# First merge weights ahead of the sample state outputs, and state transfers split by branch, on SyncE's queue

## The chip, the cores and the metric

The kernel runs on one core of a Trainium2 chip. The metric is the device time of one execution in microseconds (us); the time before is the median of three runs.

## The reference

Two layers of a hybrid decoder are applied to a prompt of 512 tokens and to a sample group of 8 sequences with 4 tokens each, with the same weights. Each layer is a half-step SwiGLU FFN, a token mixer and a second half-step FFN, each with a norm before and after. What matters here is the mixer:

```python
h = rmsnorm(x); proj = h @ w_in          # three branches and the gate logits
o_gdn, s_gdn_new = gated_delta_rule(...)  # state 4 heads x 128 x 128 per sequence
o_gla, s_gla_new = gla(...)               # state 4 x 64 x 128
o_ssd, s_ssd_new = ssd(...)               # state 8 x 64 x 128
gates = sigmoid(gate_logits + b_merge)
merged = gates[0]*(o_gdn @ w_br_gdn) + gates[1]*(o_gla @ w_br_gla) + gates[2]*(o_ssd @ w_br_ssd)
x += rmsnorm(merged @ w_out)
```

The prompt starts from zero states; the sample starts from eight given states per branch. The new states of both are outputs of the kernel.

## The kernel before, in words

Prompt and sample columns lie side by side in tiles of 128 x 544 (512 + 32). Every large product is made from fp32 weights in three passes (high x high, high x low, low x high): SyncE (SP) loads a weight block into one of four `raw` slots, GpSimd (POOL) splits it into `wh` (L494) and `wl` (L496), of which there are two slots each, and TensorE (PE) multiplies (L531, L533, L535). `lo_done` counts split blocks and frees raw slots, `blk_done` counts blocks that PE has used and frees `wh` and `wl`, and `raw_full` tells POOL that a block has landed. All engines run the same sequence of blocks.

The mixer of a layer runs in this order: the input projection (80 big loads over both layers), then a recurrent stage in which no weight is split, then 48 merge blocks of 6 k-tiles, then the output projection. In the recurrent stage each engine follows an order written out by hand (`TENSOR_ORDER`, `SCALAR_ORDER`, `VECTOR_ORDER`) over four prompt chunks and then one step for the sample. The work tiles of that stage lie over the ring of weights: `ssd_places` and the norm tiles over `raw`, `gla_places` over `wh` and `wl`. So no merge weight may be loaded before this work is over. The sample's states lie in `states` (gdn) and in columns of `proj` (`gla_states`, `ssd_states`) that the prompt's last chunk has finished with.

The semaphores `g_["s"]`, `l_["s"]` and `s_["s"]` count finished steps of the three branches: at `CHUNKS + 1` the prompt's last state of this layer is final, at `STEPS + 1` the sample's are. VectorE (DVE) writes them: L2123 (gla), L1993 (gdn) for the prompt; L2166 (gla), L2275 (ssd), L2038 (gdn) for the sample. SP's queue in a layer is, in its own order: `save_conv`, `load_states` (L431 waits for all three branches, L433 issues gdn, gla, ssd; `st_in`), `save_prompt_states` (L420, `st_prompt`), `save_states` (L438 waits and L439 issues gdn, gla, ssd; `st_out`), a wait for `st_prompt` (L465), and then the merge blocks (L401), each once `lo_done` says that its raw slot is free.

On the other side, PE's sample products wait for `st_in` at L806, L1002 and L1125 (products at L811, L1006, L1128). DVE waits for `st_prompt` at L2351 ahead of the first `hl` of the merge (L2354). PE waits for the last step of all three branches (L1216) ahead of the first merge block, and then runs six units per turn, of two blocks each: the gate's columns, then a branch's. Each unit takes two pairs of PSUM banks; from the third unit on it waits for `sg_done` and `mac_done`, which start at 2. For a unit DVE scales the gate (`sg`, L2389), ScalarE (ACT) takes its sigmoid (L1702), DVE multiplies (`mac`, `mt`, L2394) and adds (L2398). `sg`, `mt` and `mac` lie over the gdn states, so both ACT (L1695) and DVE (L2377) wait for `st_out`, all three state outputs, before the first unit.

Of the kernel before, what the change touches and what calls it, by code (L numbers as in the profile page):

```python
# [13 lines left out]
KD = D_MODEL // P  # L14
# [3 lines left out]
CHUNKS = SEQ // C  # L18
STEPS = CHUNKS + 1
# [37 lines left out]
B_MERGE = B_PROJ + 4 + 40  # L57
# [3 lines left out]
RAW, SPLIT = 4, 2  # L61
# [90 lines left out]
def trunk(nc, io):  # L152
    ctx = ExitStack()
    with ctx:
# [5 lines left out]
        def sem(name):  # L160
            return ctx.enter_context(nc.semaphore(name))
# [62 lines left out]
        def work(name, k, units=1, dt=F32):  # L224
            return at(name, R + 2048 * k, [P, 512 * units], dt)


        (kn, qn, _, _, eg, dd, aa, att, al_, xx, xt, pp, rt, rr, uu, kd, gs) = (
            work(f"g{i}", i) for i in range(17))
        kqg = at("kqg", R + 2048 * 2, [P, 2, 512])  # L230
# [35 lines left out]
        ls = gla_prompt["s"]  # L266
# [9 lines left out]
        ss_ = ssd_prompt["s"]  # L276
# [50 lines left out]
        def halves(ap):  # L327
# [21 lines left out]
        g_ = {s: sem("g_" + s) for s in (  # L349
            "xx qx xtt bc d dx brb sq ss ln rs qk kk kt eg kg at atb xi kd al p pc q x "  # L350
            "tb cx sk rt rtt r up u o oc su sm s bx mp ma sa").split()}
        l_ = {s: sem("l_" + s) for s in (
            "rc z zt a g1 gk b bt qk qe dl d1 d2 ml at cp vc vtp vt kdp kt o oc su sm s mp ma sa").split()}
        s_ = {s: sem("s_" + s) for s in (
            "bc d dx sa st tr ea ce att xd xe bt y yo yc su sm s mp skc wide").split()}
        zeroed = sem("zeroed")
        st_in = [sem(f"st_in{b}") for b in range(3)]
        st_prompt, st_out = sem("st_prompt"), sem("st_out")
# [14 lines left out]
        def value(eng, v):  # L373


            if not isinstance(v, int):
                eng.compute_val(v)
                eng.wait_ge(started, 1)
            return v
# [11 lines left out]
        @block.sync  # L391
        def _(sp_):
            sp_.dma_start(cst[:], io["cst"]).then_inc(loaded, 16)
            sp_.dma_start(x[:], io["x"].rearrange("p (k t) -> p k t", k=KD)).then_inc(loaded, 16)
            sp_.dma_start(wpre[:], io["prm"].rearrange("a p n -> p a n")[:, :, F1PRE:F1PRE + KD]).then_inc(loaded, 16)

            def blocks(layer, first, i, nks, source):

                for j, nk in enumerate(nks):
                    sp_.wait_ge(lo_done, value(sp_, layer * BLOCKS + i * len(nks) + (first + j + 1)))  # L400
                    sp_.dma_start(raw[:, j % RAW, 0:nk, :], source(j)).then_inc(raw_full[j % RAW], 16)  # L401

            def tiles(name, index):
                return io[name][bass.ds(index, 1)].rearrange("a p (k m) -> p (a k) m", m=P)

            def ups(layer, which, first, i):
                blocks(layer, first, i, (KD,) * 4, lambda j: tiles("up", layer * (2 * UPS) + i * 4 + (which * UPS + j)))

            def ffn(layer, which, first):
                with sp_.Fori(1, KF // 2) as i:  # L410
                    ups(layer, which, first, i)
                k0 = np.cumsum((0,) + DOWN_K)
                with sp_.Fori(0, 2) as i:
                    blocks(layer, first + UPS, i, DOWN_K * 4,
                           lambda j: tiles("down", layer * (2 * KD) + i * 4 + (which * KD + j // 3))
                           [:, k0[j % 3]:k0[j % 3 + 1], :])

            def save_prompt_states(layer):
                for name, cols, live in (("gdn", 512, gs), ("gla", 256, ls), ("ssd", 512, ss_)):
                    sp_.dma_start(io["out_p_" + name][bass.ds(layer, 1)].rearrange("a p n -> (a p) n"), live[:, 0:cols]).then_inc(st_prompt, 16)  # L420

            def sample_states(kind, layer):

                return ((io[kind + "gdn"][bass.ds(layer, 1)].rearrange("a p b n -> (a p) b n"), states[:, :, :]),
                        (io[kind + "gla"][bass.ds(layer, 1)].rearrange("a p (t e) n -> (a p) t (e n)", e=2), proj[:, LQ:LQ + 4, 0:512]),
                        (io[kind + "ssd"][bass.ds(layer, 1)].rearrange("a p b n -> (a p) b n"), ssd_states))

            def load_states(layer):

                for b in range(3):  # L430
                    sp_.wait_ge((g_, l_, s_)[b]["s"], value(sp_, layer * STEPS + (CHUNKS + 1)))  # L431
                for b, (outside, inside) in enumerate(sample_states("in_", layer)):
                    sp_.dma_start(inside, outside).then_inc(st_in[b], 16)  # L433

            def save_states(layer):
                for b, (outside, inside) in enumerate(sample_states("out_s_", layer)):

                    sp_.wait_ge((g_, l_, s_)[b]["s"], value(sp_, layer * STEPS + (STEPS + 1)))  # L438
                    sp_.dma_start(outside, inside).then_inc(st_out, 16)  # L439

            def save_conv(layer):

                sp_.wait_ge(conv_done, value(sp_, layer * CONV_TILES + CONV_TILES))
                sp_.wait_ge(csil_done, value(sp_, layer * CONV_TILES + CONV_TILES + 2))
                sp_.dma_start(blk[:, :, :], io["blk"].rearrange("p (l c) -> p l c", c=B)).then_inc(side_moved, 16)
                sp_.dma_start(io["out_p_conv"][bass.ds(layer, 1)].rearrange("a p t c -> (a p) t c"), cs_p[:, :, :]).then_inc(side_moved, 16)
                sp_.dma_start(io["out_s_conv"][bass.ds(layer, 1)].rearrange("a p t n -> (a p) t n"),
                              cs_s[:, :, :, :].rearrange("p t b c -> p t (b c)")).then_inc(side_moved, 16)

            for layer in range(DEPTH):  # L450

                ups(layer, 0, B_FFN1, 0)
                sp_.wait_ge(x_done, value(sp_, layer * (3 * KD) + 1))
                sp_.dma_start(prm[:], io["prm"][bass.ds(layer, 1)].rearrange("a p n -> (a p) n")).then_inc(prm_in, 16)
                ffn(layer, 0, B_FFN1)
                blocks(layer, B_PROJ, 0, (2,) * 4,
                       lambda j: tiles("narrow", layer)[:, 2 * j:2 * j + 2, :])
                with sp_.Fori(0, 10) as i:
                    blocks(layer, B_PROJ + 4, i, (KD,) * 4, lambda j: tiles("win", layer * 40 + i * 4 + j))

                save_conv(layer)
                load_states(layer)
                save_prompt_states(layer)
                save_states(layer)
                sp_.wait_ge(st_prompt, value(sp_, layer * 48 + 48))  # L465
                with sp_.Fori(0, KD // 2) as i:
                    blocks(layer, B_MERGE, i, (6, 6) * 6, lambda j: tiles("merge", layer * 48 + i * 12 + j))
                with sp_.Fori(0, 2) as i:
                    blocks(layer, B_OUT, i, (KD,) * 4, lambda j: tiles("wout", layer * KD + i * 4 + j))
                ups(layer, 1, B_FFN2, 0)  # L470
                ffn(layer, 1, B_FFN2)

            sp_.wait_ge(x_done, DEPTH * 3 * KD + 1)
            sp_.dma_start(io["y"].rearrange("p (k t) -> p k t", k=KD), x[:]).then_inc(saved, 16)
            sp_.wait_ge(saved, 16)

            sp_.wait_ge(side_moved, DEPTH * 48)
            sp_.wait_ge(st_prompt, DEPTH * 48)
            sp_.wait_ge(st_out, DEPTH * 48)
# [2067 lines left out]
```

## Time and profile before

| | us |
|---|---|
| median of 3 runs | 3475.52 (3474.49 to 3476.52) |
| the profiled execution's own time | 3466.18 |
| its span, first to last instruction | 3464.4 |
| PE busy | 3232.0 (93%) |
| POOL busy | 1570.6 (45%) |
| DVE busy | 1309.0 (38%) |
| ACT busy | 778.0 (22%) |
| mean granted TensorE clock | 0.959 |

PE is busy in nearly all of the span, so a gap in PE's work is what is to be looked for. The two recurrent stages, one per layer, stand out in the page's 40 slices: POOL is at 0 there, and at their end PE and the granted clock dip. A row of the timeline gives the start, the duration, the engine, the line, the operation with output and inputs, and in brackets how long the engine had been idle and what ended that. "SPq" is SP issuing a DMA: the duration is that of the issue, not of the transfer. A row of the windows gives the stretch and its length, then the busy time and the number of instructions of PE, PE's weight loads, DVE, ACT and POOL, then the granted clock, the busy share of the DMA engines and what they moved in GB/s. In a row of DMA landings the times are in us, while durations of instructions there are in ns (min/median/max).

### The profile page before, as it was taken

The page shows a single profiled execution, that of the slowest core. Times are in us where ns is not written, and L with a number is a line of the kernel's source. Part 1 is how long each engine was busy: PE and PEld are TensorE (multiplying, and loading weights), DVE is VectorE, ACT ScalarE, POOL GpSimd, SP SyncE. Part 2 cuts the span into 40 slices and gives each one's busy share as a digit, 9 for nine tenths or more (in the row PEclk, how much of TensorE's full clock was granted, in tenths as well). Part 3 has the DMA queues.
Part 4 walks back from the last instruction along what each step waited for, and adds up shares of the span by engine and source line. Part 5 has one row for each costly group of instructions (what it writes and reads, how often), then busy time and mean ns, then how long its engine had stood idle before and what let it go on. Part 6 is the DMA issues. An engine that isn't in the chain of part 4 may idle for free. (4 is left out here: it accounts for less than half of the span.)

```text
span 3464.4 us, 67764 instructions
## 1 busy us (share of the span) xinstructions
PE 3232.0 (93%) x26954; PEld 3109.0 (90%) x26954; DVE 1309.0 (38%) x2171; ACT 778.0 (22%) x1447; POOL 1570.6 (45%) x948
## 2 busy tenths in 40 slices
PE   7999989988869998999999999999888699899997
PEld 7999989977659998999999999899676699899997
DVE  3331075458642214331043301763777322243301
ACT  2111032244431112111021101321445311121100
POOL 4655546500016654665546554565000265546653
PEclk9999999999969999999999999999898699999999
DMA  3222222200032221222222222221001322212221
GB/s 125 85 87 83 69 81 85 84 1 2 33 130 88 92 89 63 89 85 84 75 83 85 85 84 63 88 85 66 1 2 70 107 87 88 91 62 90 85 84 64
DMA packets 77997, 259.88 MB, mean 75 GB/s; under 512 B 8576, under 2 KB 10624, under 8 KB 77056
## 3 DMA queue, kind: packets, MB, share of 16 engines
q1 hardware_dynamic: 77536, 256.90, 22.4%
q8 instruction: 131, 2.15, 0.3%
q10 hardware_dynamic: 288, 0.49, 0.1%
q14 instruction: 42, 0.34, 0.0%
HBM read 242.78 MB, written 14.58 MB: 74 GB/s over the span
## 5 line engine op out<-in xcount | busy, mean ns | idle before, releaser
L494 POOL TENSOR_SCALAR wh<-raw 128x1024 fp32r<-128x1024 f32 (+1 forms) x464 | 470.4, 1014 | 1796.5 <-PE ps L535 1139.8
L531 PE MATMUL ps<-hh,wh 128*128 128x272 f32 x4768 | 997.5, 290 | 109.7 <-POOL wl L496 51.2
L496 POOL TENSOR_TENSOR wl<-raw,wh 128x1024 fp32r<-128x1024 f32 (+1 forms) x464 | 1066.3, 2298 | 67.8 <-POOL wh L494 0.3
L533 PE MATMUL ps<-hl,wh 128*128 128x272 f32 x4768 | 992.4, 289 | 0.0
L535 PE MATMUL ps<-hh,wl 128*128 128x272 f32 x4768 | 988.1, 289 | 0.0
L531 PEld LDWEIGHTS ps<-hh,wh 128*128 128x128 f32 x4768 | 754.5, 189 | 118.2 <-issue 109.3
L535 PEld LDWEIGHTS ps<-hh,wl 128*128 128x128 f32 x4768 | 752.5, 189 | 0.0
L533 PEld LDWEIGHTS ps<-hl,wh 128*128 128x128 f32 x4768 | 752.1, 189 | 0.0
L531 PE MATMUL ps<-ah,wh 128*128 128x272 f32 x1408 | 294.5, 291 | 0.0
L1760 DVE SCALAR_TENSOR_TENSOR f<-f,prm,rstd_post 128x544 f32<-128x544 f32 x48 | 43.7, 916 | 653.7 <-ACT rstd_post L1260 653.7
L533 PE MATMUL ps<-al,wh 128*128 128x272 f32 x1408 | 290.2, 287 | 0.0
L535 PE MATMUL ps<-ah,wl 128*128 128x272 f32 x1408 | 289.4, 287 | 0.0
L1793 DVE TENSOR_TENSOR prod<-sil,ps 128x544 f32<-128x544 f32 x88 | 63.5, 722 | 440.4 <-PE ps L535 431.5
L531 PEld LDWEIGHTS ps<-ah,wh 128*128 128x128 f32 x1408 | 221.8, 188 | 1.9
L535 PEld LDWEIGHTS ps<-ah,wl 128*128 128x128 f32 x1408 | 220.8, 188 | 0.0
L533 PEld LDWEIGHTS ps<-al,wh 128*128 128x128 f32 x1408 | 220.2, 188 | 0.0
L1799 DVE TENSOR_TENSOR al<-prod,ah 128x544 f32 x88 | 148.7, 1690 | 97.1 <-ACT ah L1304 97.1
L1820 DVE SCALAR_TENSOR_TENSOR cacc<-pad,cw,cacc 128x568 f32<-128x568 f32 x120 | 160.7, 1339 | 12.5
L1304 ACT ACTIVATE ah<-prod 128x544 f32 x88 | 58.1, 660 | 470.8 <-DVE prod L1795 470.8
L1290 ACT ACTIVATE sq<-ps 128x544 f32<-128x544 f32 x48 | 30.0, 624 | 588.1 <-PE ps L535 588.1
L2389 DVE TENSOR_TENSOR sg<-ps,rstd 128x544 f32<-128x544 f32 x48 | 34.8, 724 | 276.5 <-PE ps L535 276.5
L1790 DVE TENSOR_TENSOR sil<-ps,rstd 128x544 f32<-128x544 f32 x88 | 63.7, 724 | 176.0 <-PE ps L535 128.5
(421 smaller groups left out, 3689.1 us busy)
## 6 DMA issues: line engine op xcount, KB each, us to landing
raw<-in_up SPq DMA_DIRECT2D x176, 512.0 KB, 3.5
raw<-in_win SPq DMA_DIRECT2D x80, 512.0 KB, 3.5
raw<-in_merge SPq DMA_DIRECT2D x96, 384.0 KB, 3.0
raw<-in_down SPq DMA_DIRECT2D x64, 512.0 KB, 3.5
raw<-in_down SPq DMA_DIRECT2D x32, 384.0 KB, 3.1
raw<-in_wout SPq DMA_DIRECT2D x16, 512.0 KB, 3.5
states<-in_in_gdn SPq DMA_DIRECT2D x2, 2048.0 KB, 8.2
proj<-in_in_ssd SPq DMA_DIRECT2D x2, 2048.0 KB, 16.2
```

The costliest lines, as they stand in the source:

```text
L494: pool.tensor_scalar(hi, src, 1.0, 1.0, MULT, MULT).then_inc(hi_done, 1)
L496: pool.tensor_tensor(lo, src, hi.bitcast(F32), SUB).then_inc(lo_done, 1)
L531: pe.matmul(out, high, mh_[:, c], start=a, stop=False)
L533: pe.matmul(out, high, ml_[:, c], start=False, stop=False)
L535: last = pe.matmul(out, low, mh_[:, c], start=False, stop=b)
L1304: act.activation(ah[:, bass.ds(i * 2 + j, 1), :].rearrange("p k t -> p (k t)"), prod[:, j, :], ACT.Copy).then_inc(ah_done, 1)
L1760: dve.scalar_tensor_tensor(out=f[:, k, :], in0=f[:, k, :], scalar=prm[:, wcol + k:wcol + k + 1], in1=rstd_post[:, :], op0=MULT, op1=MULT). ...
L1790: dve.tensor_tensor(halves(sil[:, j, :]), pair(2 * j), halves(rstd[:, :]), MULT).then_inc(gate_done, 1)
L1793: dve.tensor_tensor(halves(prod[:, j, :]), halves(sil[:, j, :]), pair(2 * j + 1), MULT).then_inc(prod_tmp, 1)
L1799: dve.tensor_tensor(al[:, m, :].rearrange("p k t -> p (k t)"), prod[:, j, :], ah[:, m, :].rearrange("p k t -> p (k t)").bitcast(F32), SUB) ...
L1820: last = dve.scalar_tensor_tensor(out=a, in0=pad[:, j, t:t + CW], scalar=cw[:, 4 * j + t:4 * j + t + 1], in1=a, op0=MULT, op1=ADD)
L2389: dve.tensor_tensor(halves(sg[:, u % 2, :]), pair(2 * u % 4), halves(rstd[:, :]), MULT).then_inc(gate_done, 1)
```

## The change

On SP's queue only:

1. The sample's state loads and the prompt's state outputs go branch by branch: gdn and gla loads and the gla prompt output once gla's prompt part is done; the ssd load and the gdn prompt output once gdn's is done; then the ssd prompt output. Before, all waited for all three branches.
2. The first four merge blocks (`RAW` slots) are requested ahead of the sample's state outputs, once ssd's and gla's sample steps are over, with the wait for `st_prompt` ahead of them. Then come the state outputs, now in the order gla, ssd, gdn, and then the other merge blocks. The first turn of twelve blocks is taken out of the hardware loop to make this possible.

No other engine's instructions change.

```diff
-            def blocks(layer, first, i, nks, source):
+            def blocks(layer, first, i, nks, source, part=slice(None)):
-                for j, nk in enumerate(nks):
+                for j, nk in list(enumerate(nks))[part]:
...
-            def load_states(layer):
-                for b in range(3):
-                    sp_.wait_ge((g_, l_, s_)[b]["s"], value(sp_, layer * STEPS + (CHUNKS + 1)))
-                for b, (outside, inside) in enumerate(sample_states("in_", layer)):
-                    sp_.dma_start(inside, outside).then_inc(st_in[b], 16)
+            def turn_states(layer):
+                (gdn_out, gdn_in), (gla_out, gla_in), (ssd_out, ssd_in) = sample_states("in_", layer)
+                sp_.wait_ge(l_["s"], layer * STEPS + (CHUNKS + 1))
+                sp_.dma_start(gdn_in, gdn_out).then_inc(st_in[0], 16)
+                sp_.dma_start(gla_in, gla_out).then_inc(st_in[1], 16)
+                save_prompt_state(layer, "gla", 256, ls)
+                sp_.wait_ge(g_["s"], layer * STEPS + (CHUNKS + 1))
+                sp_.dma_start(ssd_in, ssd_out).then_inc(st_in[2], 16)
+                save_prompt_state(layer, "gdn", 512, gs)
+                sp_.wait_ge(s_["s"], layer * STEPS + (CHUNKS + 1))
+                save_prompt_state(layer, "ssd", 512, ss_)
...
             def save_states(layer):
-                for b, (outside, inside) in enumerate(sample_states("out_s_", layer)):
+                out = sample_states("out_s_", layer)
+                for b in (1, 2, 0):
+                    outside, inside = out[b]
...
-                load_states(layer)
-                save_prompt_states(layer)
+                turn_states(layer)
+                def merges(i, part=slice(None)):
+                    blocks(layer, B_MERGE, i, (6, 6) * 6, lambda j: tiles("merge", layer * 48 + i * 12 + j), part)
+                for e in (l_, s_):
+                    sp_.wait_ge(e["s"], layer * STEPS + (STEPS + 1))
+                sp_.wait_ge(st_prompt, layer * 48 + 48)
+                merges(0, slice(0, RAW))
                 save_states(layer)
-                sp_.wait_ge(st_prompt, value(sp_, layer * 48 + 48))
-                with sp_.Fori(0, KD // 2) as i:
-                    blocks(layer, B_MERGE, i, (6, 6) * 6, lambda j: tiles("merge", layer * 48 + i * 12 + j))
+                merges(0, slice(RAW, 12))
+                with sp_.Fori(1, KD // 2) as i:
+                    merges(i)
```

## Rows read from the trace of the kernel before

**Rows 1.** The page: busy time, share of the span and instructions by engine.
```profile
PE 3232.0 (93%) x26954; PEld 3109.0 (90%) x26954; DVE 1309.0 (38%) x2171; ACT 778.0 (22%) x1447; POOL 1570.6 (45%) x948
```

**Rows 2.** Windows around both layers' first merge block.
```profile
980.00:1001.00 21.00, 18.34 (x167) 14.31 (x165) 18.26 (x39) 11.27 (x30) 0.00 (x0) 0.50 0.01 2
...
1002.30:1026.40 24.10, 0.10 (x2) 0.00 (x0) 5.75 (x13) 0.79 (x2) 2.82 (x3) 0.50 0.76 283
...
1026.40:1029.40 3.00, 2.94 (x13) 2.97 (x14) 0.00 (x0) 0.00 (x0) 2.43 (x2) 0.52 0.45 131
...
2743.80:2749.60 5.80, 5.71 (x25) 5.75 (x26) 0.00 (x0) 0.00 (x0) 2.46 (x2) 0.50 0.47 138
```

**Rows 3.** Timeline of layer 0, from the end of the sample step to the first merge block.
```profile
1002.95 1.28 DVE L2275 TENSOR_TENSOR proj<-proj,ps 128x512 f32<-128x512 f32 x2
1004.15 2.47 DVE L2038 TENSOR_TENSOR states<-states,ps 128x512 f32<-128x512 f32 x4
1006.65 0.33 SPq L439 DMA_DIRECT2D res_out_s_gdn<-states  x1
1007.24 0.69 DVE L2297 TENSOR_TENSOR ol<-nt_s,oh 128x128 fp32r<-128x128 f32 x3
...
1022.19 0.16 DVE L2381 COPY bm<-prm 128x6 f32<-128x6 f32 x1 [14.26 <-DMA res_out_s_ssd<-proj]
1023.43 0.83 POOL L494 TENSOR_SCALAR wh<-raw 128x768 fp32r<-128x768 f32 x1 [322.11 <-DMA raw<-in_merge]
...
1026.46 0.79 PE L531 MATMUL ps<-hh,wh 128*128 128x272 f32 x2 [24.07 <-POOL wl L496]
```

**Rows 4.** Layer 1: timeline (one row), then the chain that ended last (start, us, what).
```profile
2719.88 1.29 DVE L2275 TENSOR_TENSOR proj<-proj,ps 128x512 f32<-128x512 f32 x2
...
2726.46 14.10 DMA raw<-in_merge
...
2743.89 0.79 PE ps L531 x2
```

**Rows 5.** Loads to landing: merge (all; layer 0's first), down; the page's list (median).
```profile
L401 SPq DMA_DIRECT2D raw<-in_merge x96: 332/333/4199, 1009.5 to 2938.9; - x96
DMA to landing us min/median/max: 2.7/3.0/14.1
...
DMA to landing us min/median/max: 13.6/13.6/13.6
...
DMA to landing us min/median/max: 2.9/3.4/5.0
states<-in_in_gdn SPq DMA_DIRECT2D x2, 2048.0 KB, 8.2
proj<-in_in_ssd SPq DMA_DIRECT2D x2, 2048.0 KB, 16.2
res_out_s_gdn<-states SPq DMA_DIRECT2D x2, 2048.0 KB, 6.5
res_out_s_ssd<-proj SPq DMA_DIRECT2D x2, 2048.0 KB, 14.8
```

**Rows 6.** Layer 0's state loads, the products on them, `hl` (its line's own view).
```profile
944.17 0.34 SPq L433 DMA_DIRECT2D states<-in_in_gdn  x1
955.66 1.93 PE L811 MATMUL ps<-states,kqs 128*8 128x128 f32 x64
...
L2354 DVE SCALAR_TENSOR_TENSOR hl<-x,prm,hh x16: 776/779/784, 985.5 to 2723.5; 128x544 fp32r<-128x544 f32 x16
```

**Rows 7.** POOL, DVE and ACT in layer 0's first merge units, from the timeline.
```profile
1046.05 0.83 POOL L494 TENSOR_SCALAR wh<-raw 128x768 fp32r<-128x768 f32 x1 [1.65 <-PE ps L535]
1059.49 1.15 POOL L494 TENSOR_SCALAR wh<-raw 128x768 fp32r<-128x768 f32 x1 [1.65 <-PE ps L535]
1036.97 0.73 DVE L2389 TENSOR_TENSOR sg<-ps,rstd 128x544 f32<-128x544 f32 x1 [14.62 <-PE ps L535]
1039.09 0.75 ACT L1702 ACTIVATE sg<-sg,bm 128x544 f32<-128x544 f32 x1
```

More of the change, by code:

```diff
@@ L416, in ffn, with save_prompt_state @@
                            [:, k0[j % 3]:k0[j % 3 + 1], :])
-            def save_prompt_states(layer):
-                for name, cols, live in (("gdn", 512, gs), ("gla", 256, ls), ("ssd", 512, ss_)):
-                    sp_.dma_start(io["out_p_" + name][bass.ds(layer, 1)].rearrange("a p n -> (a p) n"), live[:, 0:cols]).then_inc(st_prompt, 16)
+            def save_prompt_state(layer, name, cols, live):
+                sp_.dma_start(io["out_p_" + name][bass.ds(layer, 1)].rearrange("a p n -> (a p) n"), live[:, 0:cols]).then_inc(st_prompt, 16)
             def sample_states(kind, layer):
@@ L426, in sample_states @@
                         (io[kind + "ssd"][bass.ds(layer, 1)].rearrange("a p b n -> (a p) b n"), ssd_states))
-            def load_states(layer):
-                for b in range(3):
-                    sp_.wait_ge((g_, l_, s_)[b]["s"], value(sp_, layer * STEPS + (CHUNKS + 1)))
-                for b, (outside, inside) in enumerate(sample_states("in_", layer)):
-                    sp_.dma_start(inside, outside).then_inc(st_in[b], 16)
+            def turn_states(layer):
[9 more added lines that the diff above has]
+                save_prompt_state(layer, "ssd", 512, ss_)
             def save_states(layer):
-                for b, (outside, inside) in enumerate(sample_states("out_s_", layer)):
-                    sp_.wait_ge((g_, l_, s_)[b]["s"], value(sp_, layer * STEPS + (STEPS + 1)))
+                out = sample_states("out_s_", layer)
+                for b in (1, 2, 0):
+                    outside, inside = out[b]
+                    sp_.wait_ge((g_, l_, s_)[b]["s"], layer * STEPS + (STEPS + 1))
                     sp_.dma_start(outside, inside).then_inc(st_out, 16)
```

## The prediction

> **What bounds the kernel now.** I read the page first. PE is busy 93% of the span and POOL, which feeds it, 45% [rows 1]: outside a few gaps the kernel runs at the pace of PE's large products, so only a gap of PE, or a wait on the way into one, is worth anything. The windows show where such a gap lies. Between the sample step and the first merge block PE does 0.10 us of work in 24.1 us, while the DMA engines are 76% busy at 283 GB/s [rows 2]. The timeline tells what is late in it. DVE ends the last state of ssd at 1004.23 (1002.95 + 1.28) and the last of gdn at 1006.62; SP issues the first state output 0.03 us later, at 1006.65; POOL starts on the first merge block at 1023.43, after 322 us of idleness ended by that block's load, and PE follows at 1026.46 [rows 3]. Layer 1 repeats it: ssd ends at 2721.17, PE starts at 2743.89, and the load alone, from 2726.46 on, is 14.10 us of the chain that ended last [rows 4]. A merge load usually lands 3.0 us after its issue; layer 0's first takes 13.6 us and layer 1's 14.1 us [rows 5]. It is issued behind 5 MB of state outputs and lands behind them. That queueing, plus the wait for gdn, which the slots do not need, is what the change goes for.
>
> **Part 1, merge blocks first.** In layer 0 SP is now released by ssd's last state at 1004.23 instead of gdn's at 1006.62; gla's last is earlier. With the same 0.03 us the load is issued at 1004.26 and, with nothing ahead of it, lands after 3.0 us. From the landing on I take before's path as it is: 1009.55 + 13.6 = 1023.15 was the landing (the issue ended the SP work that began at 1006.65, and the first merge issue stands at 1009.5 in the rows), POOL began 0.28 us later and PE 3.03 us after POOL [rows 3, 5]. So PE starts at 1004.26 + 3.0 + 0.28 + 3.03 = 1010.6, against 1026.46: **15.9 us**. Layer 1: 2721.17 + 0.03 + 3.0 + 0.28 + 3.03 = 2727.5 against 2743.89: **16.4 us** [rows 4]. Together 32.3 us, all of it on PE's path, as nothing else works for PE in that gap.
>
> The other inputs of the first block are there in time: gdn's last state, for which PE waits too, at 1006.62, and the last sample part of `ol` at 1007.24 + 0.69 = 1007.93 [rows 3]. That leaves 2.7 us of cover; without it, PE would start that much later.
>
> Bounds of the load: 2.7 us is the fastest merge load; 5.0 us is the slowest in the down products, where a load shares the queue with its neighbours [rows 5], as here the first shares it with three more issued 0.36 us apart (an issue takes 0.33). I take 3.0, the median, since the first goes first; the ends give -0.6 and +4.0 us over both layers. POOL's split now overlaps DVE's last 0.4 us: a split row that ran beside other work took 1.15 against 0.83 us [rows 7], so 0 to +0.3 us each; I take 0.
>
> **Clock.** After the gap PE begins at the lower level (1.2 GHz, granted 0.50 to 0.52) and stays there for some 3.0 us in layer 0 and 5.8 us in layer 1 before it is granted 2.4 GHz; the level was already 0.50 in the last 21 us of the sample step, before the gap [rows 2]. So a gap of 8 us instead of 24 does not spare the climb. It costs half of the low time, 1.5 and 2.9 us, and I keep both; if the new low times are both like the shorter or both like the longer, that is -1.4 or +1.4 us in total.
>
> **What is late next.** The outputs and the fifth block now come behind four blocks. Before, the outputs took 1022.19 - 1006.65 = 15.5 us from first issue to last landing, and the first merge block landed 1.0 us after them, which I take as the time of one block [rows 3, 5]. Now: 1004.26 + 4 x 1.0 + 15.5 = 1023.8 for `st_out`, and 1024.8 for the fifth block. PE's first four blocks last from 1026.46 to 1046.05, 19.6 us with the climb (POOL's sixth split, at 1046.05, is released by the end of PE's fourth block [rows 7]), so PE is through with them at 1010.6 + 19.6 = 1030.2. The fifth block must have landed 0.28 + 2.75 us (one split) earlier, by 1027.2: 2.4 us of cover. The third unit also needs the first gate's sigmoid: from DVE's start on it to ACT's end were 1039.84 - 1036.97 = 2.87 us [rows 7], and 0.2 for the copy before, so `st_out` must be there by 1027.1: 3.3 us of cover. Both hold, neither widely; what either overshoots PE would lose once per layer. If PE's climb is short its fourth block ends earlier and eats the cover, so a lucky clock gains less than it seems.
>
> **Part 2, state transfers by branch.** Gdn's and gla's loads now go when gla's prompt part is done, ahead of 944.17. Nobody waited for them: gdn's load, issued at 944.17 and landing 8.2 us later by the page's list of issues, is there at 952.4 [rows 5, 6], and PE's first product on it starts at 955.66, released by DVE's work and not by the load [rows 6]; gla's and ssd's products come after it in PE's order, behind several others. I cost it at 0. Its gain is at most 0.3 us per layer (what a wait for the load could hide in that start), and I bound its loss, if the traffic slowed the serial end of the last chunk (the 7 us before 944.17), by the same 0.3: POOL's first split, in a window with the DMA engines 45% busy, took 0.83 us like a later one [rows 2, 3, 7], so traffic of that kind did not slow an engine. The prompt outputs go earlier or, gdn's, less than 1 us earlier; DVE's first `hl`, which needs them, starts at 985.5 [rows 6], and SP itself waits for them at 1004; both are over 20 us behind what the queue holds after 944.17 (the ssd load's 16.2 us [rows 5] and 0.6 MB more). The turn unrolled on SP and the constant waits cost SP some tens of ns per block where it has microseconds. All at 0.
>
> **Sum.** 15.9 + 16.4 = 32.3 us off the profiled execution's 3466.18 us: 3433.9 (span 3464.4 to 3432.1). The median of the runs lies 9.3 us above that execution; the gain is a wait taken out, and I take it to be the same there: 3475.5 - 32.3 = **3443.2 us**.
>
> **Rivals.** *A: the supply of the fifth block or `st_out` becomes the wait.* The cover is 2.4 us at 1 us per block; for it speaks that merge issues behind the outputs were held up to 4.2 us in SP [rows 5], which says that the queue is full. An overshoot of 3 us per layer gives 3449.2. *B: the order of requests does not set the order of landings*, as transfers in flight together share the engines. Then the first block lands up to as late as the last output: 1004.26 + 19.5 + 0.4 = 1024.2 against 1023.15, so +1.0 us per layer, 3477.6, about no change. Against it: the gdn output, issued first, landed after 6.5 us and the ssd output after 14.8 [rows 5], so what is first in this queue does finish first. The Trainium skill, "DMA: Bandwidth & Descriptors", section "Two DMAs through the same engine are not ordered", says that descriptors of one queue start in order but are pipelined, and that a later transfer may complete before an earlier one; by a strict reading asking first would buy nothing certain, and the sum would be B's 3477.6. The trace shows order kept at this size. *C: SP is not released earlier*, since gdn's state is still waited for: the change would bring the queueing alone, 2.4 us less per layer, 3448.0. The diff names only gla and ssd in that wait, which speaks against it. *D, slower: the clock does not climb.* In the sample step PE was busy 18.34 of 21 us and stayed at 0.50 [rows 2], so being busy alone does not raise it. If PE, coming out of a short gap, stayed low through the first four blocks, they would cost some 4 x 4.48 = 17.9 us more (4.48 is (1059.49 - 1046.05) / 3 [rows 7]) against 1.5 now: about even with the 15.9 gained, and that is the point from which it decides. Through eight blocks in both layers it is 2 x 35.8 - 4.4 - 32.3 = +34.9 us, 3510. Against it: both climbs here came within 5.8 us of the same products.
>
> **Chances.** Forecast, 3439.5 to 3447: 0.74. A, up to 3452: 0.12. C: 0.03. A gain some us larger, from the shorter bounds together and a sample step that profits: 0.04. B: 0.04. D: 0.03. The range that should hold 8 times in 10 is 3438.5 to 3452. A difference under 0.2% (7 us) can't be told from none; so faster 0.93, same 0.04 (B), slower 0.03 (D).
>
> **What would show it.** Right: SP's first merge issue some 0.03 us after DVE's last L2275 and before its last L2038; the largest merge landing around 3 us for the first block and long ones only for the fifth and later; PE idle before its first merge block down from 24.1 to about 8.3 us; POOL's fifth split released by PE and not by a DMA; DVE's copy at L2381 released by the gdn output, now the last, 19 to 20 us after the first merge issue. Wrong: the first block landing after the outputs (B); a wait of POOL for the fifth load or of PE for ACT's `sg` (A); a granted clock of 0.50 beyond the first block and a half (D); the stretch from 937 to 1004 longer or shorter by over 0.5 us (part 2).

## The result, and the profile after

The changed kernel takes 3437.94 us (median of four runs, 3435.02 to 3440.83) against 3475.01 us for the kernel before (four runs) in the same comparison: a ratio of 0.9893, 95% interval 0.9876 to 0.9910. In a second comparison, with 17 runs of the kernel before (median 3470.66, 3464.08 to 3476.49) and five of the changed one (median 3437.16), it is 0.9903 (0.9888 to 0.9918). The forecast was 3443.2 us with a range from 3438.5: faster, as forecast, but just below the range. The profiled execution took 3440.28 us (span 3438.5).

The page after: the span of this execution is 25.9 us shorter, PE's busy time is 4.8 us longer (3236.8 against 3232.0), and POOL's wait for merge loads is still there, since POOL has nothing to do in the recurrent stage. The longer busy time goes with more time at the lower clock in this execution (see "Where the scatter sits").

```profile
span 3438.5 us, 67666 instructions
PE 3236.8 (94%) x26954; PEld 3112.6 (91%) x26954; DVE 1313.0 (38%) x2171; ACT 777.7 (23%) x1447; POOL 1573.1 (46%) x948
```

Lines of the code below the edit are 16 higher than before: L2291 is before's L2275 (last ssd state), L2054 is L2038 (gdn state), L510 and L512 are POOL's split, L547 to L551 the products. The timeline of layer 0 at the same place as in [rows 3]:

```profile
1001.18 1.29 DVE L2291 TENSOR_TENSOR proj<-proj,ps 128x512 f32<-128x512 f32 x2
1002.38 2.47 DVE L2054 TENSOR_TENSOR states<-states,ps 128x512 f32<-128x512 f32 x4
1002.53 1.76 SPq L401 DMA_DIRECT2D raw<-in_merge  x4
1004.34 0.62 SPq L448 DMA_DIRECT2D res_out_s_gla<-proj  x1
1005.01 0.67 SPq L448 DMA_DIRECT2D res_out_s_ssd<-proj  x1
1005.72 3.95 SPq L448 DMA_DIRECT2D res_out_s_gdn<-states  x1
1006.08 0.83 POOL L510 TENSOR_SCALAR wh<-raw 128x768 fp32r<-128x768 f32 x1 [304.98 <-DMA raw<-in_merge]
1009.12 0.79 PE L547 MATMUL ps<-hh,wh 128*128 128x272 f32 x2 [8.49 <-POOL wl L512]
1022.94 0.16 DVE L2397 COPY bm<-prm 128x6 f32<-128x6 f32 x1 [16.78 <-DMA res_out_s_gdn<-states]
```

The reader is to see four things. SP issues the merge loads 0.06 us after the last ssd state (1002.47), while gdn's is still being made. POOL starts 3.55 us after the issue instead of 13.9. PE's idle time ahead of its first merge block is 8.49 us instead of 24.07. And `st_out` is complete 20.4 us after the first merge issue. Everything here stands 1.8 us earlier than the prediction's absolute times (1002.47 for 1004.23), since the recurrent stage of layer 0 was 1.7 us shorter in this execution. That stage took 324.4 to 328.6 us in four executions of the kernel before, and 322.7 to 330.2 us over all kernels and both layers, so the difference is scatter.

Layer 1, from the waits (us in total, times, longest):

```profile
PE ps L547 <- POOL wl L512: 8.4, 1, 8.4
POOL wh L510 <- DMA raw<-in_merge: 315.0, 2, 312.1
```

and its fifth and sixth splits from POOL's timeline:

```profile
2733.87 0.84 POOL L510 TENSOR_SCALAR wh<-raw 128x768 fp32r<-128x768 f32 x1 [2.85 <-DMA raw<-in_merge]
2737.15 0.84 POOL L510 TENSOR_SCALAR wh<-raw 128x768 fp32r<-128x768 f32 x1 [0.44 <-PE ps L551]
```

Here POOL waits 2.85 us for a second load, the fifth block, which it did not in layer 0. PE does not wait for it: it ends its fourth block at 2737.15, when POOL has been done with that split for 0.44 us (its idle time in the second row). In layer 1 the cover of the fifth block was used up to within half a microsecond.

The landings of layer 0's first four merge loads (min, median, max in us), and of the gdn output of both layers. Each transfer adds 16 to its semaphore, and a row takes the first 16 counts as the landing of the first transfer on that semaphore, the next 16 as that of the second, and so on. The three state outputs share `st_out`, so their rows are in order by the way they are counted; only the last of them, which stands for all 48, is sure:

```profile
DMA to landing us min/median/max: 3.3/4.8/6.2
...
DMA to landing us min/median/max: 17.2/17.6/18.1
```

### The profile page after: what moved, and what is told of

It is laid out like the page before. It is cut to its first block and busy times, and to the rows that moved or that the text cites. A ratio compares the mean times of both kernels' runs of the same rounds, so it can differ in the third digit from the quotient of the medians.

```text
span 3438.5 us, 67666 instructions
## 1 busy us (share of the span) xinstructions
PE 3236.8 (94%) x26954; PEld 3112.6 (91%) x26954; DVE 1313.0 (38%) x2171; ACT 777.7 (23%) x1447; POOL 1573.1 (46%) x948
## 5 line engine op out<-in xcount | busy, mean ns | idle before, releaser
L510 POOL TENSOR_SCALAR wh<-raw 128x1024 fp32r<-128x1024 f32 (+1 forms) x464 | 473.0, 1019 | 1768.1 <-PE ps L551 1136.5
L512 POOL TENSOR_TENSOR wl<-raw,wh 128x1024 fp32r<-128x1024 f32 (+1 forms) x464 | 1066.4, 2298 | 67.9 <-POOL wh L510 0.3
L547 PE MATMUL ps<-hh,wh 128*128 128x272 f32 x4768 | 997.5, 291 | 78.5 <-DVE hl L1767 44.6
L551 PE MATMUL ps<-hh,wl 128*128 128x272 f32 x4768 | 987.9, 289 | 0.0
L547 PEld LDWEIGHTS ps<-hh,wh 128*128 128x128 f32 x4768 | 754.6, 189 | 87.1 <-issue 78.3
L551 PEld LDWEIGHTS ps<-hh,wl 128*128 128x128 f32 x4768 | 752.3, 189 | 0.0
L547 PE MATMUL ps<-ah,wh 128*128 128x272 f32 x1408 | 294.8, 291 | 0.0
L551 PE MATMUL ps<-ah,wl 128*128 128x272 f32 x1408 | 289.8, 287 | 0.0
L547 PEld LDWEIGHTS ps<-ah,wh 128*128 128x128 f32 x1408 | 222.2, 188 | 1.9
L551 PEld LDWEIGHTS ps<-ah,wl 128*128 128x128 f32 x1408 | 221.1, 188 | 0.0
L1836 DVE SCALAR_TENSOR_TENSOR cacc<-pad,cw,cacc 128x568 f32<-128x568 f32 x120 | 151.1, 1259 | 12.5
## 6 DMA issues: line engine op xcount, KB each, us to landing
proj<-in_in_ssd SPq DMA_DIRECT2D x2, 2048.0 KB, 10.4
```

Of the source, the lines that this page charges most:

```text
L510: pool.tensor_scalar(hi, src, 1.0, 1.0, MULT, MULT).then_inc(hi_done, 1)
L512: pool.tensor_tensor(lo, src, hi.bitcast(F32), SUB).then_inc(lo_done, 1)
L547: pe.matmul(out, high, mh_[:, c], start=a, stop=False)
L551: last = pe.matmul(out, low, mh_[:, c], start=False, stop=b)
L1836: last = dve.scalar_tensor_tensor(out=a, in0=pad[:, j, t:t + CW], scalar=cw[:, 4 * j + t:4 * j + t + 1], in1=a, op0=MULT, op1=ADD)
```

## The experiments

Two theories stood at the outset. **W**: the gain is the wait removed, 31 to 32 us, and the rest of the difference to 37 us is scatter of both kernels, from where in the recurrent stages the granted clock is low. **S**: the branch-wise state transfers bring the missing 5 us.

### The changed kernel again, and each part alone

The changed kernel, unaltered:

> The changed kernel once more, to see how its times scatter beside those of the kernel before. Theory W (the gain is the wait of PE ahead of the first merge block, and the rest of the difference is where in the recurrent stages the granted clock is low): in the profile PE starts its first merge block 6.6 us after the last ssd state in both layers (15.6 to 16.4 us less than before), and the times scatter by some 5 us between executions, with a mean gain of 32 to 40 us. Rival S (the split of the state transfers by branch gains some us by itself): the gain over the kernel before is 37 us in all runs and the sample step is shorter than before's 66.7 us in both layers.

Part 1 alone (the state transfers all wait for the three branches, as before):

```diff
-                sp_.wait_ge(l_["s"], layer * STEPS + (CHUNKS + 1))
...
+                for b in range(3):
+                    sp_.wait_ge((g_, l_, s_)[b]["s"], layer * STEPS + (CHUNKS + 1))
+                for b, (outside, inside) in enumerate(sample_states("in_", layer)):
+                    sp_.dma_start(inside, outside).then_inc(st_in[b], 16)
+                for name, cols, live in (("gdn", 512, gs), ("gla", 256, ls), ("ssd", 512, ss_)):
+                    save_prompt_state(layer, name, cols, live)
```

> Part 1 alone: the first four merge blocks ahead of the state outputs, the state loads and prompt outputs all together as before. Theory W: the same as the changed kernel within the 5 us scatter, a gain of 32 to 40 us. Rival S: 4 to 6 us slower than the changed kernel, a gain of about 32 us.

Part 2 alone (branch-wise transfers kept, outputs and merge blocks in the old order):

```diff
-                for b in (1, 2, 0):
+                for b in (0, 1, 2):
...
-                for e in (l_, s_):
-                    sp_.wait_ge(e["s"], layer * STEPS + (STEPS + 1))
+                save_states(layer)
                 sp_.wait_ge(st_prompt, layer * 48 + 48)
-                merges(0, slice(0, RAW))
-                save_states(layer)
-                merges(0, slice(RAW, 12))
+                merges(0)
```

> Part 2 alone: state loads and prompt outputs by branch; the sample outputs and merge blocks in the old order. Theory W: no change against the kernel before, within the scatter of 5 us; PE's gap ahead of the first merge block stays at 24 us. Rival S: a gain of 4 to 6 us.

| kernel | median us (runs) | lowest to highest | ratio to before, 95% interval |
|---|---|---|---|
| before | 3470.66 (17) | 3464.08 to 3476.49 | |
| changed, again | 3437.16 (5) | 3432.61 to 3439.73 | 0.9903 (0.9888 to 0.9918) |
| part 1 alone | 3437.44 (5) | 3430.08 to 3441.81 | 0.9901 (0.9884 to 0.9918) |
| part 2 alone | 3470.26 (12) | 3465.88 to 3474.13 | 0.9997 (0.9989 to 1.0006) |

S falls: part 2 brings 0.0003 of the time, with an interval that ends at 0.11% (3.8 us, below the 4 to 6 us of S), and part 1 alone is the whole gain. Nor is the sample step shorter, as S had it: from gla's last prompt state to ssd's last sample state it took 66.7 us in layer 0 and 70.0 us in layer 1 of the changed kernel's first execution, and 66.7 in both layers before. With part 2 alone PE's gap is where it was (layer 0):

```profile
PE ps L544 <- POOL wl L509: 24.1, 1, 24.1
DVE bm L2394 <- DMA res_out_s_ssd<-proj: 14.3, 1, 14.3
```

In the second execution of the changed kernel the gaps are 8.2 and 8.2 us, so the gaps of two executions are 31.8 and 32.3 us below before's. The gain between the medians, 33.5 us (3470.66 to 3437.16), lies near that.

### The release by ssd instead of gdn

```diff
-                for e in (l_, s_):
+                for e in (g_, l_, s_):
                     sp_.wait_ge(e["s"], layer * STEPS + (STEPS + 1))
```

> The changed kernel, but the first four merge blocks wait for gdn's last state too. Theory W: PE starts its first merge block 2.4 us later per layer, the gap is 10.9 us instead of 8.5, and the time is 4.8 us above the changed kernel's. If the earlier release did not matter (the load bound by something else): no difference.

Median 3442.33 us of five (3437.43 to 3443.64), 5.2 us above the changed kernel on the same chip. The gaps, of layer 0 and of layer 1:

```profile
PE ps L547 <- POOL wl L512: 10.6, 1, 10.6
...
PE ps L547 <- POOL wl L512: 10.7, 1, 10.7
```

That is 2.1 to 2.5 us more each than in the two executions of the changed kernel: the earlier release is worth what the prediction charged for it (2.4 per layer), and rival C, by which it would not happen, is the state of this kernel and not of the changed one. The gaps show this, the times alone do not: the runs of the two kernels overlap, and so do the intervals of their ratios (0.9917, 0.9902 to 0.9932, against 0.9888 to 0.9918).

### One block ahead instead of four

```diff
-                merges(0, slice(0, RAW))
+                merges(0, slice(0, 1))
                 save_states(layer)
-                merges(0, slice(RAW, 12))
+                merges(0, slice(1, 12))
```

> The changed kernel, but only one merge block, not four, is asked for ahead of the state outputs. Theory (what lands behind the outputs lands some 20 us after the first request, and the four slots are what covers that): the second block lands some 17 us after the first output's issue, PE waits about 8 us for it in each layer, and 16 us of the gain are given back: about 3453. Rival (the outputs and later loads pass each other in the queue, so one block ahead is enough): the same time as the changed kernel, 3437, with no second wait.

3461.29 us (seven runs, 3457.05 to 3465.63; ratio 0.9968, 0.9957 to 0.9980, where the changed kernel has 0.9903). Of some 33 us of gain 23 are given back, more than the 16 expected. POOL's timeline and PE's waits in layer 0:

```profile
1012.82 0.97 POOL L510 TENSOR_SCALAR wh<-raw 128x768 fp32r<-128x768 f32 x1 [311.68 <-DMA raw<-in_merge]
1029.33 0.83 POOL L510 TENSOR_SCALAR wh<-raw 128x768 fp32r<-128x768 f32 x1 [13.59 <-DMA raw<-in_merge]
```

```profile
PE ps L547 <- issue: 10.0, 1, 10.0
PE ps L547 <- POOL wl L512: 8.4, 1, 8.4
```

The first gap is as short as in the changed kernel, and a second one of 10.0 us (9.6 in layer 1) stands behind the first block: what is asked for behind the outputs lands behind them. That is 19.6 us of new gaps. The rest is the clock. Once more it is at the lower level, from 1026.0 to 1036.2, some 4 us of it behind the gap that ends at 1032.2, where the changed kernel stays at the upper one:

```profile
1026.00:1032.50 6.50, 0.29 (x1) 0.32 (x2) 0.16 (x1) 0.00 (x0) 3.02 (x3) 0.50 0.56 215
1032.50:1036.20 3.70, 3.70 (x18) 3.70 (x18) 0.00 (x0) 0.00 (x0) 2.23 (x2) 0.50 0.51 123
1036.20:1038.00 1.80, 1.80 (x16) 1.80 (x16) 0.00 (x0) 0.00 (x0) 0.00 (x0) 1.00 0.47 184
```

At half price that is 2 us, and as much in layer 1. By this estimate 19.6 + 4 agrees with the 23 lost. The direction and the mechanism were right and the price was too low: the second block landed as late as it did because it was issued 3.3 us after the first, behind the three outputs, and a gap costs itself and a climb.

### How far the gap can be cut

Three kernels cut the 8.5 us further. The first asks for the first block as soon as the last scaling of the ssd state has read the work tile under its slot:

```diff
-                for e in (l_, s_):
-                    sp_.wait_ge(e["s"], layer * STEPS + (STEPS + 1))
+                sp_.wait_ge(l_["s"], layer * STEPS + (STEPS + 1))
                 sp_.wait_ge(st_prompt, layer * 48 + 48)
-                merges(0, slice(0, RAW))
+                sp_.wait_ge(s_["sm"], layer * (CHUNKS + 4) + CHUNKS + 4)
+                merges(0, slice(0, 1))
+                sp_.wait_ge(s_["s"], layer * STEPS + (STEPS + 1))
+                merges(0, slice(1, RAW))
```

> The first merge block is requested once the last scaling of the ssd state (the last reader of the work tile under the first raw slot) is done, 1.3 us before the last ssd state; the other three as in the changed kernel. Theory (the gap is the path release, load, split): PE's gap ahead of the first merge block falls from 8.5 to 7.2 us, 2.6 us in all, 3434.5. Rival (the load is bound by something else in that stretch): the gap stays.

The second leaves SP alone and lets PE start on the high half; the new function runs the products of `wh` with `hh` and `hl` over the six tiles, waits for `lo_done`, and then runs those of `wl` with `hh`:

```diff
-                        product(layer, B_MERGE, i, 2 * u, 12, 2 * u % 4, 6, h_tiles, True, False,
-                                ready=h_split(layer, 2) if i is FIRST and u == 0 else None)
+                        if i is FIRST and u == 0:
+                            pe.wait_ge(hi_done, layer * BLOCKS + B_MERGE + 1)
+                            first_gate(layer)
+                        else:
+                            product(layer, B_MERGE, i, 2 * u, 12, 2 * u % 4, 6, h_tiles, True, False)
```

> The changed kernel, but in the first merge block PE runs all products with the high half of the weights first, as soon as POOL has written that half, and the low half's products after them. Theory: PE starts 1.95 us earlier per layer (gap 6.5 us instead of 8.5) and its high products cover the low half's split, 3.9 us in all, 3433. Rival: PE's earlier start is spent at the lower clock or in a new wait for the low half, and the time stays.

The third does both:

> Both of the last two. Theory: the gap is 5.2 us and the time 6.5 us below the changed kernel's, about 3430.5, unless gdn's last state, for which PE waits too, comes first (it is done 0.9 us before the start expected here).

| kernel | gaps of PE, layer 0 and 1 | profiled span | median us (4 runs each) | lowest to highest |
|---|---|---|---|---|
| changed | 8.5, 8.4 | 3438.5 | 3437.94 | 3435.02 to 3440.83 |
| first slot early | 7.2, 7.2 | 3438.1 | 3437.90 | 3434.04 to 3441.52 |
| high half first | 6.5, 6.3 | 3432.0 | 3433.78 | 3431.33 to 3442.30 |
| both | 4.8, 5.0 | 3432.5 | 3438.54 | 3434.31 to 3440.22 |

The gaps came out as expected to 0.4 us. The times that went with them in the expectations (3434.5, 3433 and 3430.5 us) did not, except the second, and they can't decide: each kernel's four runs scatter over 6 to 11 us, so expected differences of 2.6 to 6.5 us between medians can't be read, and no gain of these three over the changed kernel is shown by its time. The traces show that part of what is cut comes back. With both, layer 0, PE's wait and POOL's timeline:

```profile
PE ps L1241 <- POOL wh L512: 4.8, 1, 4.8
```

```profile
1028.56 0.83 POOL L512 TENSOR_SCALAR wh<-raw 128x768 fp32r<-128x768 f32 x1 [3.78 <-DMA raw<-in_merge]
```

The second is the fifth block: POOL waits 3.78 us for it, and now PE waits too, 0.7 us in layer 0 and 1.0 in layer 1 (0.8 and 1.4 with the high half first alone). This is the prediction's rival A, come true once PE starts still earlier.

### Relief for the fifth block

On top of both: behind the four blocks only gdn's output, which alone lies under the gate's tiles, then two more blocks, then gla's and ssd's outputs on a semaphore of their own, for which ACT waits ahead of its first `mh` (under ssd's states).

```diff
-                save_states(layer)
-                merges(0, slice(RAW, 12))
+                save_states(layer, (0,))
+                merges(0, slice(RAW, RAW + 2))
+                save_states(layer, (1, 2))
+                merges(0, slice(RAW + 2, 12))
...
-                act.wait_ge(st_out, layer * 48 + 48)
+                act.wait_ge(st_out, layer * 16 + 16)
...
+                            if i == 0 and u == 2:
+                                act.wait_ge(st_late, layer * 32 + 32)
```

> The last kernel (high half first, first slot early), and behind its four merge blocks only gdn's output (the only one that lies under the gate's tiles), then two more merge blocks as their slots come free, then gla's and ssd's outputs, with a semaphore of their own that ACT waits for ahead of its first write over those states. Theory (with the gap cut, the fifth block's landing behind 5 MB of outputs is the next wait, some 1 to 2 us per layer): POOL's fifth split is released by PE and not by the load, in both layers, and the time is 2 to 4 us below the last kernel's. Rival (the fifth block is not what is late): the time is the same, and POOL's fifth split is where it was relative to its first.

3429.63 us (four runs, 3426.43 to 3432.69); ratio to before 0.9880 (0.9864 to 0.9897). The fifth block's split is now released by PE in both layers (layer 0's row):

```profile
1025.88 0.83 POOL L515 TENSOR_SCALAR wh<-raw 128x768 fp32r<-128x768 f32 x1 [1.70 <-PE ps L556]
```

and at the start of the merge PE waits for nothing but the first block, 5.1 and 4.9 us. Its median is the lowest of the study, and its slowest run is faster than eight of the changed kernel's nine, though the intervals of the two ratios still overlap (0.9864 to 0.9897 against 0.9888 to 0.9918). Against the kernel with both cuts its waits of PE are shorter by 11.5 - 10.0 = 1.5 us, and its median by 8.9 (2 to 4 were expected), beside medians of the kernel before of 3470.77 and 3470.91; the 1.5 us are shown, and what the other 7 are is not.

### Where the scatter sits

> The kernel before, for one more profile. Theory (the scatter of 12 us between executions is the granted clock in the recurrent stages and sample steps): the spans differ by about half of what the time at the lower clock differs in the stretches from the last projection load to the last sample state; the stretches of large products agree within 1 us or so. Rival (it comes from the large products or the DMA queue): those stretches differ by several us.

> The kernel before once more. As for the first look: the stretches of large products agree within 1 us and the recurrent stages differ with the time at the lower clock, or else the large products differ by several us.

> The kernel before a third time. As for the first look: the stretches of large products agree within 1 us and the recurrent stages differ with the time at the lower clock, or else the large products differ by several us.

The table cuts four executions of the kernel before and two of the changed one at events that they share: the first load after the last projection block, PE's last product ahead of the gap, and its first merge product. In brackets is the time at the lower clock in the stretch, summed from the trace's records.

| execution | span | layer 0 recurrent | layer 1 recurrent | large products, between | large products, end |
|---|---|---|---|---|---|
| before, first | 3464.4 | 324.4 (78.9) | 325.1 (82.4) | 1367.7 (33.5) | 720.5 (31.0) |
| before, second | 3473.0 | 325.7 (82.7) | 327.5 (87.5) | 1370.2 (36.6) | 722.2 (29.3) |
| before, third | 3470.7 | 328.0 (90.8) | 327.5 (87.5) | 1368.7 (35.2) | 719.1 (29.6) |
| before, fourth | 3469.5 | 328.6 (90.9) | 323.9 (79.0) | 1367.3 (31.8) | 723.1 (30.2) |
| changed, first | 3438.5 | 322.7 (75.5) | 330.2 (94.3) | 1369.7 (35.5) | 721.1 (28.1) |
| changed, again | 3433.1 | 323.8 (79.0) | 327.6 (87.5) | 1369.2 (35.7) | 718.5 (25.6) |

The windows show it for the execution that the prediction was read from, and for the third of the kernel before. The columns are those of [rows 2]; the number that changes is the clock, 0.88 and 0.87 against 0.86 and 0.87:

```profile
678.00:1002.40 324.40, 278.16 (x3097) 231.10 (x3096) 215.77 (x599) 146.64 (x318) 13.78 (x8) 0.88 0.06 23
2394.20:2719.30 325.10, 280.04 (x3097) 232.60 (x3096) 215.72 (x599) 146.60 (x318) 13.74 (x8) 0.87 0.06 23
...
678.60:1006.60 328.00, 282.79 (x3097) 233.59 (x3095) 215.14 (x599) 146.68 (x317) 13.80 (x8) 0.86 0.06 22
2399.40:2726.90 327.50, 282.11 (x3098) 234.24 (x3096) 215.79 (x599) 146.59 (x317) 13.78 (x8) 0.87 0.06 22
```

DVE and ACT do the same work in the same time to 0.7 us; only PE's busy time is longer. The recurrent stretches follow their low time almost exactly: 75.5 us low goes with 322.7 us, 79 with 323.8 to 324.4, 82.5 with 325.1 to 325.7, 87.5 with 327.2 to 327.6, 91 with 328.0 to 328.8, 94.3 with 329.6 to 330.2, in the fourteen profiled executions of this study, whichever kernel; the one of 28 stretches that stands off this line does so by 1.5 us (84.0 with 327.6, where 84.1 went with 325.9 and 326.2). That is 7.5 us for 18.8 us of low time, 0.40 us per us: about the half expected. That it is a little less because PE is not always what is waited for is likely and not shown. The large products are not as quiet as the theory had it: between the stages the four executions of the kernel before differ by 2.9 us (1367.3 to 1370.2) and at the end by 4.0 us (719.1 to 723.1), without the low time to explain the latter. Against the first execution the other three are 8.6, 6.3 and 5.1 us longer, and the recurrent stages bring 3.7, 6.0 and 3.0 us of that; in the second, the large products bring more (4.2 us). So the clock in the recurrent stages goes with the larger part of the scatter, some 13 of 20 us over these three, the second theory is half right, and what moves the last stretch by 4 us stays open.

## Why the prediction was right or wrong

**The gap.** Right. The release came 0.06 us after ssd's last state (0.03 taken), the load took 3.3 us (3.0), POOL started 0.25 us after its landing and PE 3.04 us after POOL (0.28 and 3.03). From the last ssd state to PE it took 6.65 us for 6.34. Both gaps together fell from 48.7 to 16.9 us, by 31.8 us for the 32.3 forecast. The two profiled executions differ by 25.9 us only, and the table closes that too: the recurrent stages of the changed kernel's were 3.4 us longer and its large products 2.6 us, and 31.8 - 6.0 = 25.8. The two ends set for the load, 2.7 and 5.0 us, held it. POOL's first split took 0.83 us beside DVE in layer 0 and 1.00 in layer 1, within the 0.3 allowed.

**The clock.** Right in kind. It was at 0.50 before the gap, in it and behind it:

```profile
1000.60:1009.10 8.50, 0.03 (x2) 0.01 (x1) 5.53 (x11) 0.73 (x2) 2.87 (x3) 0.50 0.60 173
1009.10:1013.90 4.80, 4.78 (x21) 4.80 (x22) 0.00 (x0) 0.00 (x0) 2.39 (x2) 0.50 1.05 409
1013.90:1016.20 2.30, 2.30 (x20) 2.30 (x19) 0.00 (x0) 0.00 (x0) 0.02 (x1) 1.00 1.05 409
```

PE's low time was 4.8 us in layer 0 and 3.1 in layer 1, 7.9 in all for 8.8 before. Rival D (no climb) did not occur in any execution.

**What is late next.** The places were right, and the cover was thinner than reckoned in layer 1 alone. `st_out` was complete 20.4 and 21.5 us after the first merge issue, forecast 19.5; the fifth block landed about 21 and 22 us after it, forecast 20.5. The term that was too small seems to be the time per block in the queue, 1.0 us, which was taken from a load behind the outputs: the first of the four landed at 1002.5 + 3.3 = 1005.8 and the last at 1003.9 + 6.2 = 1010.1, so 1.4 us apart. In layer 0 PE's first four blocks took 20.6 us and not 19.6, which gave the cover back: the fifth block was there 3.0 us before it was due, forecast 2.4. In layer 1 POOL waited for the fifth load, which is the sign that the prediction set for rival A, and 0.44 us were left ahead of PE. PE did not wait in the changed kernel, but in layer 1 only just; rival A is what the kernels with the shorter gap met.

**Order of landings.** Rival B is rejected by the timeline after: the last of the four blocks landed at 1010.1, and the first output, gla's, at 1004.34 + 8.4 = 1012.7 (8.4 is its row in the page's list of issues). The blocks have semaphores of their own (`raw_full`), so this order is not one of counting. But the prediction's argument against B was not sound: that the gdn output landed after 6.5 us and the ssd output after 14.8 says nothing of their order, since both are counted on `st_out`. And its sentence "The trace shows order kept at this size" goes too far. In the same trace of the kernel before, layer 0, the ssd load (2 MB, issued at 945.3, on a semaphore of its own) landed at 945.3 + 17.0 = 962.3, while the first 16 counts of the prompt outputs, all issued behind it (the first, of 256 KB, at 946.5), were there at 946.5 + 13.8 = 960.3:

```profile
L433 SPq DMA_DIRECT2D proj<-in_in_ssd x1: 1170/1170/1170, 945.3 to 945.3; - x1
DMA to landing us min/median/max: 17.0/17.0/17.0
...
L420 SPq DMA_DIRECT2D res_out_p_gdn<-g x1: 5312/5312/5312, 946.5 to 946.5; - x1
DMA to landing us min/median/max: 13.8/13.8/13.8
```

So part of what was asked for later was done first, by 2 us. This agrees with the rule of the Trainium skill that the prediction cites ("DMA: Bandwidth & Descriptors", section "Two DMAs through the same engine are not ordered"): the order is not promised. That four blocks asked for ahead of 5 MB land ahead of them is what these traces show, and no more.

**Part 2.** Right: 0 forecast, 0.9997 measured. The ssd load, which now goes as soon as gdn's prompt state is final, some 6 us behind the other two loads, landed after 10.4 us instead of 16.2, and nobody had waited for it. The sign that the prediction set for part 2, the stretch from 937 to 1004 changed by over 0.5 us, was a bad one: it is 66.7 us in layer 0 before and after, but 70.0 us in layer 1 after, and 70.0 us in layer 0 of the third execution of the kernel before too, where nothing was changed.

**The base, where the prediction failed.** The step is "The median of the runs lies 9.3 us above that execution; the gain is a wait taken out, and I take it to be the same there", with the range built on it. The subtraction was sound, the base of 3475.5 was not. Three runs within 2 us looked like a firm median and the profiled 3466.2 like an oddity of profiling. In the three later comparisons the kernel before has its median at 3470.7, 3470.9 and 3470.8 us, with 34 runs from 3464.1 to 3477.0, and the profiled execution lies inside that range. From 3470.7 the same sum gives 3438.4, which is 0.5 us from the first median of the changed kernel and 1.2 from the second. By the medians of the first comparison the gain was 37.1 us, 5 us more than the gaps gave back, and by those of the second 33.5. The range of -4.7 us held the errors of the terms only and had no term for the base; 9.3 us between a profile and the runs was the sign that one of at least 5 us to each side belonged in it. The prediction asked of the clock only what it does to the climb behind the gap and not what it does in the 325 us ahead of it, where it is low for a quarter of the time.

Why the first runs were high is not shown. All four runs of the kernel before in the first comparison lie at 3474.1 or above, and of those 34 later ones only four do, so chance alone would seldom give it. The changed kernel's four runs beside them were not high (3437.94 against 3437.16 later). None of those four runs of the kernel before was profiled, so where they spent the 5 us is not on record.

**Rival C.** Rejected by the SP row at 1002.53, ahead of gdn's last state; the kernel that waits for gdn shows its price.

## What to carry to other kernels

A load that gates the busiest engine belongs ahead of bulk outputs in a shared queue, and as many of its successors with it as will be used before the bulk has landed: one ahead gave back 23 of 33 us. After such a move, work out when the next load and the outputs' own waiters come due, since cover of 2 or 3 us vanished here with the next cut. A row that gives landings on a shared semaphore can't tell which transfer was first. And before a forecast takes a median as its base, set the profile's time beside the runs: if they differ by more than the runs do among themselves, the scatter is at least that difference, and stages where the clock comes and goes are the place to look.

## What the runs showed of the hardware that was not expected

The recurrent stage's length is nearly a function of its time at the lower clock, 0.40 us per us of it over fourteen executions, and which parts of it are low differs from execution to execution of the same kernel. The longest and the shortest of these stages differ by 7.5 us, 0.2% of the kernel.

Short operations of DVE stretched where POOL's ran beside them. In the kernel with the first slot early, layer 0, the three small `ol` subtractions took 2.92 us instead of 0.69, and POOL's `wl` beside them 2.08 instead of 1.80:

```profile
1009.73 2.08 POOL L514 TENSOR_TENSOR wl<-raw,wh 128x768 fp32r<-128x768 f32 x1
1010.08 2.92 DVE L2315 TENSOR_TENSOR ol<-nt_s,oh 128x128 fp32r<-128x128 f32 x3
1011.78 0.87 POOL L512 TENSOR_SCALAR wh<-raw 128x768 fp32r<-128x768 f32 x1
...
L2315 DVE TENSOR_TENSOR ol<-nt_s,oh x3: 280/904/1884, 1010.1 to 1012.7; 128x128 fp32r<-128x128 f32 x3
```

One by one they took 1.88, 0.90 and 0.28 us. The first ended at 1011.96, 0.15 us after POOL's `wl`, the second at 1012.79, 0.14 us after POOL's next `wh`, and the third, which began behind that, took its usual time. So each `ol` that began beside an operation of POOL ended just behind it. The forecast had allowed 0.3 us for POOL's side of such overlap, which is what POOL's `wl` took more, and nothing for DVE's. Here PE needed `ol` only for its second block and did not wait for it; a cut that brings the two together ahead of a waiting PE would pay some 2 us, by an estimate from these rows (2.92 - 0.69).
